# Gathering experts after four heads' choice instead of eight, with the weight remainders on VectorE

## What is computed

```
def peer_mixer(h, w_q, keys_1, keys_2, u_tab, v_tab):
    q = (hf @ w_q).reshape(t, PEER_HEADS, PEER_QUERY_DIM)
    s1 = jnp.einsum('thd,nd->thn', q[..., :half], keys_1)
    s2 = jnp.einsum('thd,nd->thn', q[..., half:], keys_2)
    v1, i1 = lax.top_k(s1, PEER_TOPK)
    v2, i2 = lax.top_k(s2, PEER_TOPK)
    cand = (v1[..., :, None] + v2[..., None, :]).reshape(t, PEER_HEADS, PEER_TOPK * PEER_TOPK)
    sc, ci = lax.top_k(cand, PEER_TOPK)
    ...
    experts = (e1 * PEER_N_KEYS + e2).reshape(t, PEER_HEADS * PEER_TOPK)
    gates = jax.nn.softmax(sc, axis=-1)
    def expert_block(args):
        a = jax.nn.gelu(jnp.einsum('td,ted->te', hb, u_tab[eb]), approximate=False)
        w = (gb * a)
        return jnp.einsum('te,ted->td', w, v_tab[eb])
```

## Time and profile before

| what | value |
|---|---|
| median of 3 runs | 2500.1 us (2497.99 to 2506.24) |
| the profiled execution | 2501.13 us, its span 2499.4 us |
| mean granted TensorE clock | 0.914 |
| busy, share of the span | PE 82%, DVE 63%, POOL 50%, ACT 40% |
| DMA | 726.60 MB, of which 540.59 MB by the indirect queue |

### The profile page before, as it was taken

How to read it: one execution, slowest core, us unless ns; L and a number is a source line. 1 busy time by engine, 2 the same in 40 slices (tenths; PEclk the granted TensorE clock), 3 DMA queues, 4 the chain that set the end, 5 groups by cost and what they waited for, 6 DMA issues and landing times. The chain is left out here.

```text
span 2499.4 us, 22306 instructions
## 1 busy us (share of the span) xinstructions
PE 2057.0 (82%) x7187; PEld 1278.5 (51%) x7187; DVE 1575.2 (63%) x2938; ACT 992.7 (40%) x2294; POOL 1251.8 (50%) x800
## 2 busy tenths in 40 slices
PE   5997867378999777777699888888999969687999
PEld 3785645244554232322356444445665647455787
DVE  4648546888886577765779875667887852452111
ACT  4215443133333222223453568445343334344443
POOL 3532000075765353444477444567898847004887
PEclk8986678689999899999899999899999989788999
DMA  7630035299999999999899999999999955003564
GB/s 263 232 121 1 1 133 152 93 419 406 420 420 405 421 421 421 422 421 421 350 358 377 409 404 344 377 378 380 419 418 407 418 208 155 26 1 93 171 191 153
DMA packets 128640, 726.60 MB, mean 291 GB/s; under 512 B 14471, under 2 KB 15498, under 8 KB 62986
## 3 DMA queue, kind: packets, MB, share of 16 engines
q0 software_dynamic: 74800, 540.59, 53.0%
q1 hardware_dynamic: 53088, 184.44, 21.2%
q10 hardware_dynamic: 634, 0.14, 0.0%
HBM read 716.45 MB, written 8.66 MB: 290 GB/s over the span
## 5 line engine op out<-in xcount | busy, mean ns | idle before, releaser
L1326 PE MATMUL ps<-uv_ring_a,expert_diag_a 128*128 128x512 f32 x1920 | 918.0, 624 | 232.9 <-ACT expert_diag_a L1308 214.6
L1107 POOL DMA_INDIRECT uv_ring_a<-in_peer_uv_dram,expert_idx x512 | 620.3, 1212 | 647.1 <-PE ps L1326 510.9
L1254 DVE CUSTOM_DVE_ANT_0 uv_ring_a<-uv_ring_a,x_rows 128x1024 f32<-128x1024 f32 x512 | 787.1, 1544 | 248.4 <-DMA uv_ring_a<-in_peer_uv_dram,expert_idx 246.8
L1326 PEld LDWEIGHTS ps<-uv_ring_a,expert_diag_a 128*128 128x128 f32 x1920 | 368.9, 198 | 699.9 <-issue 369.4
L1401 POOL TENSOR_TENSOR w_low_a<-w_raw_a,w_high_a 128x1024 fp32r<-128x1024 f32 x122 | 302.1, 2477 | 109.9 <-ACT w_high_a L1393 108.0
L1401 POOL TENSOR_TENSOR w_low_b<-w_raw_b,w_high_b 128x1024 fp32r<-128x1024 f32 x98 | 233.9, 2390 | 228.5 <-ACT w_high_b L1393 227.1
L1293 ACT ACTIVATE expert_gelu_a<-expert_dot_a 128x2 f32<-128x2 f32 x256 | 52.1, 204 | 691.0 <-DVE expert_dot_a L1254 690.7
L1393 ACT CAST w_high_a<-w_raw_a 128x1024 fp32r<-128x1024 f32 x146 | 152.0, 1042 | 192.5 <-PE ps L1414 172.5
L1308 ACT ACTIVATE expert_diag_a<-ident,expert_weight_a 128x128 f32<-128x128 f32 x480 | 168.5, 395 | 0.6 <-ACT expert_weight_a L1299 0.4
L1393 ACT CAST w_high_b<-w_raw_b 128x1024 fp32r<-128x1024 f32 x98 | 102.9, 1051 | 116.8 <-PE ps L1414 114.5
L1299 ACT ACTIVATE expert_weight_a<-expert_gelu_a,expert_gate 128x1 f32<-128x1 f32 x512 | 122.9, 286 | 8.6
(11 more groups left out here) (463 smaller groups left out, 3334.5 us busy)
## 6 DMA issues: line engine op xcount, KB each, us to landing
w_raw_a<-in_w_gu_dram SPq DMA_DIRECT2D x44, 512.0 KB, 7.8
w_raw_b<-in_w_gu_dram SPq DMA_DIRECT2D x44, 512.0 KB, 3.6
w_raw_a<-in_w_peer_q_dram SPq DMA_DIRECT2D x32, 512.0 KB, 7.1
w_raw_a<-in_w_out_dram SPq DMA_DIRECT2D x24, 512.0 KB, 7.7
w_raw_a<-in_w_in_dram SPq DMA_DIRECT2D x24, 512.0 KB, 6.2
w_raw_b<-in_w_in_dram SPq DMA_DIRECT2D x24, 512.0 KB, 3.8
w_raw_a<-in_w_down_dram SPq DMA_DIRECT2D x22, 512.0 KB, 7.8
w_raw_b<-in_w_down_dram SPq DMA_DIRECT2D x22, 512.0 KB, 3.6
```

Source lines behind the costliest of these rows:

```text
L1107: pool.indirect_dma_start(out=self.ring[:, n % self.RING, :], out_offset=None, in_=K.uv, in_offset=bass.IndirectOffsetOnAxis(ap=K.idx[self ...
L1254: dve.tensor_tensor_reduce(u, u, self.h[b][:, :], 1.0, 0.0, ALU.mult, ALU.add, self.a[:, s:s + 1]).then_inc(self.s_dot, 1)
L1326: ins = nc.tensor.matmul(self.bank(half), self.diag[q % self.DIAGS][:, :], self.ring[:, n % self.RING, D + 512 * half:D + 512 * half + 512 ...
```

## The change

It has five pieces.

- **Choice in groups of four.** `HG` goes from 2 to 4. Ahead of the first dot product only heads 0 to 3 of block 0 are chosen, and their gates made. Heads 4 to 7 are chosen during the first slots (204 steps of choice over 100 slots in block 0, for those heads and the next block), their gates at slot 42. The exponential and the gates are made in halves.
- **Scores loaded behind weight tiles.** For block 1 the first score load is placed after the first weight tile of `tail_b`, the second at the place of slot 36.
- **`tail_b` starts 3 slots later**, at `at(6)`.
- **All remainders of the first stage on DVE.** The 122 tiles of L1401 leave POOL's queue, which then holds indirect DMAs alone.
- **The front.** ACT writes `h_high` in one pass from the normalised row; DVE makes `h` itself (`tensor_scalar`, L513 of the changed kernel) and then the remainder; PE waits slice by slice for column tile 0.

```diff
@@ Columns.turned @@
+            if ready:
+                pe.wait_ge(ready, k + 1)
...
@@ stage_front: scalar, tensor, vector @@
-                act.activation(K.hT[:, k, :], K.hT[:, k, :], ACT.Identity, scale=K.g1[:, k:k + 1],
-                               bias=shift[k]).then_inc(s_h, 1)
-                act.wait_ge(s_h, k + 1)
-                act.copy(hi[:, k, :], K.hT[:, k, :]).then_inc(s_hh, 1)
+                act.activation(hi[:, k, :], K.hT[:, k, :], ACT.Identity, scale=K.g1[:, k:k + 1],
+                               bias=shift[k]).then_inc(s_hh, 1)
...
-                    w.turned(pe, n, K.ps[n % 2][:, :], x)
+                    w.turned(pe, n, K.ps[n % 2][:, :], x, ready=None if n else s_hl)
...
+                dve.tensor_scalar(K.hT[:, k, :], K.hT[:, k, :], K.g1[:, k:k + 1], shift[k], ALU.mult, ALU.add).then_inc(s_h, 1)
+                dve.wait_ge(s_h, k + 1)
                 dve.tensor_tensor(lo[:, k, :], K.hT[:, k, :], hi[:, k, :].bitcast(F32), ALU.subtract).then_inc(s_hl, 1)
@@ Gather @@
-    G, DIAGS, HG = 2, 4, 2
+    G, DIAGS, HG = 2, 4, 4
...
-                yield max(self.at((r - 2) * SLOTS + 44 * (hg + 1) + 4), tail.end + 4.0 + hg)
-                sp.wait_ge(self.s_swf, self.GROUPS * (r - 1) + 2 * hg + 2)
+                if r == 1:
+                    yield self.at(36) if hg else self.start - 1.0
+                else:
+                    yield max(self.at((r - 2) * SLOTS + 44 * (hg + 1) + 4), tail.end + 4.0 + hg)
+                sp.wait_ge(self.s_swf, self.GROUPS * (r - 1) + hg + 1)
...
-        for n in range(self.GROUPS * per + 1):
-            yield tail.scored[min(n // per, self.GROUPS - 1)] + 0.25 * (n % per)
-            next(first, None)
-        yield tail.end + 11.0
-        gates(0)
+        for n in range(per):
+            yield tail.scored[1] + 0.25 * n
+            next(first)
+        yield tail.scored[1] + 0.25 * per + 2.0
+        gates(0, 0)
...
+                if b == 0:
+                    ahead, steps, over = chain(first, ahead), steps + per, 100
...
-            while done * 88 < steps * (s + 1) and done <= steps:
+            while done * over < steps * (s + 1) and done <= steps:
                 next(ahead, None)
                 done += 1
+            if s == 42 and b == 0:
+                gates(0, 1)
...
-            if s == 0:
-                act.wait_ge(self.s_gate, b + 1)
+            if s % self.WIDE == 0:
+                act.wait_ge(self.s_gate, self.GROUPS * b + s // self.WIDE + 1)
...
+            if g == 19:
+                exps(0, 1)
@@ stage_first @@
-            plan.us = g.at(3)
+            plan.us = g.at(6)
...
-            weave(rows_in(pool), g.pool(pool), W.lows(pool, dense))
+            weave(rows_in(pool), g.pool(pool))
...
-            weave(g.dve(dve), W.lows(dve, 0, dense), bias.dve(dve), half.dve(dve, begin + 80.0), *(n.dve(dve, [(s_later, 16)]) for n in ahead),
+            weave(g.dve(dve), W.lows(dve), bias.dve(dve), half.dve(dve, begin + 80.0), *(n.dve(dve, [(s_later, 16)]) for n in ahead),
```

More of the change, by code:

```diff
@@ L9 @@
 from contextlib import ExitStack
+from itertools import chain
 F32 = mybir.dt.float32
@@ L203, in lows, with turned @@
                                self.hi[n % self.SPLIT][:, :].bitcast(F32), ALU.subtract).then_inc(self.s_lo, 1)
-    def turned(self, pe, n, bank, x, cols=P):
+    def turned(self, pe, n, bank, x, cols=P, ready=None):
         hi, lo = (t[n % self.SPLIT][:, :].rearrange("p (k c) -> p k c", k=KD) for t in (self.hi, self.lo))
@@ L442, in _ @@
             for n in range(VG):
-                if n == 0:
-                    pe.wait_ge(s_hl, KD)
-                else:
-                    if n >= 2:
-                        pe.wait_ge(*out(n - 2))
+                if n >= 2:
+                    pe.wait_ge(*out(n - 2))
                 if n == A:
@@ L1018 @@
 class Gather:
-    G, DIAGS, HG = 2, 4, 2
+    G, DIAGS, HG = 2, 4, 4
     GROUPS = PEER_H // HG
+    WIDE = HG * TOPK
     def __init__(self, K, ctx, blocks, rows, start, us, banks, ring, share=0, own=0):
@@ L1184, in route @@
             dve.wait_ge(self.s_idx, self.GROUPS * r + hg + 1)
+            den = self.den[:, HG * hg:HG * hg + HG]
+            ch.link(dve.tensor_copy(den, top[:, :, 0:1].rearrange("p a b -> p (a b)")))
+            dve.tensor_tensor(top, top, den.unsqueeze(2).to_broadcast([P, HG, TOPK]), ALU.subtract).then_inc(self.s_d, 1)
             yield
-        top = self.top[:, :, :]
-        ch.link(dve.tensor_copy(self.den[:, :], self.top[:, :, 0:1].rearrange("p a b -> p (a b)")))
-        dve.tensor_tensor(top, top, self.den[:, :].unsqueeze(2).to_broadcast([P, PEER_H, TOPK]),
-                          ALU.subtract).then_inc(self.s_d, 1)
-        yield
     def dve(self, dve):
@@ L1194, in dve, with gates @@
         ch = Chain(dve, self.s_dve)
-        def gates(r):
-            dve.wait_ge(self.s_e, r + 1)
-            g = K.gate[self.blocks[r] % 2][:, :].rearrange("p (h a) -> p h a", h=PEER_H)
-            ch.link(dve.tensor_reduce(self.den[:, :], g, AX_X, ALU.add))
-            ch.link(dve.reciprocal(self.den[:, :], self.den[:, :]))
-            dve.tensor_tensor(g, g, self.den[:, :].unsqueeze(2).to_broadcast([P, PEER_H, TOPK]),
-                              ALU.mult).then_inc(self.s_gate, 1)
+        def gates(r, hg):
+            dve.wait_ge(self.s_e, self.GROUPS * r + hg + 1)
+            g = K.gate[self.blocks[r] % 2][:, self.WIDE * hg:self.WIDE * (hg + 1)].rearrange("p (h a) -> p h a", h=self.HG)
+            den = self.den[:, self.HG * hg:self.HG * (hg + 1)]
+            ch.link(dve.tensor_reduce(den, g, AX_X, ALU.add))
+            ch.link(dve.reciprocal(den, den))
+            dve.tensor_tensor(g, g, den.unsqueeze(2).to_broadcast([P, self.HG, TOPK]), ALU.mult).then_inc(self.s_gate, 1)
         def add(n):
@@ L1247, in dve @@
             if s == 0:
-                ahead = self.route(dve, ch, r) if r < len(self.blocks) else iter(())
                 routing, done = r < len(self.blocks), 0
-                steps = self.GROUPS * per + 1
+                ahead = self.route(dve, ch, r) if routing else iter(())
+                steps, over = self.GROUPS * per, 88
+                if b == 0:
+                    ahead, steps, over = chain(first, ahead), steps + per, 100
                 dve.wait_ge(self.tails[b // 2].s_h, 4)
@@ L1255, in dve @@
                                      self.a[:, s:s + 1]).then_inc(self.s_dot, 1)
-            while done * 88 < steps * (s + 1) and done <= steps:
+            while done * over < steps * (s + 1) and done <= steps:
                 next(ahead, None)
                 done += 1
+            if s == 42 and b == 0:
+                gates(0, 1)
             if s == 110 and routing:
-                gates(r)
+                for hg in range(self.GROUPS):
+                    gates(r, hg)
                 r += 1
@@ L1279, in act, with exps @@
         per = SLOTS // G
-        def exps(r):
-            act.wait_ge(self.s_d, r + 1)
-            act.activation(K.gate[self.blocks[r] % 2][:, :], self.top[:, :, :].rearrange("p a b -> p (a b)"),
+        def exps(r, hg):
+            act.wait_ge(self.s_d, self.GROUPS * r + hg + 1)
+            act.activation(K.gate[self.blocks[r] % 2][:, self.WIDE * hg:self.WIDE * (hg + 1)],
+                           self.top[:, self.HG * hg:self.HG * (hg + 1), :].rearrange("p a b -> p (a b)"),
                            ACT.Exp).then_inc(self.s_e, 1)
-        yield self.tails[0].end + 10.0
-        exps(0)
+        yield self.tails[0].scored[1] + 0.25 * (15 * self.HG + 8) + 1.0
+        exps(0, 0)
         r = 1
@@ L1309, in act @@
                                scale=self.w[:, i:i + 1]).then_inc(self.s_diag, 1)
+            if g == 19:
+                exps(0, 1)
             if g % per == 52 and r < len(self.blocks):
-                exps(r)
+                for hg in range(self.GROUPS):
+                    exps(r, hg)
                 r += 1
```

9 lines of the change are left out of this document (4 added, 5 removed).

## The result

The changed kernel took 2476.7 us (2468.14 to 2478.64), the kernel before 2499.1 on the same chip: ratio 0.991 (0.9888 to 0.9933), some 22 us faster. Six more executions of it (the run `again`) gave 2471.6 and 0.9896 (0.9873 to 0.9918). The forecast was 2467, its range 2440 to 2489.

The account below looks back on a forecast made before the run. The gather's transfers, at a ceiling of 421 GB/s, were taken to bound the stage, so only an earlier start or fuller stretches help. -8 - 20 + 3 - 5 - 3 = -33 from the median 2500.1 gave 2467 us, range 2440 to 2489.

Parts of the forecast that it names:

- The front: Before the first stage: tile 0 and everything behind it come sooner, -8 us, bounds -5 and -9.
- The start: Start of the gather: transfers full at about 468 instead of 500, -20 us, bounds -13 and -26.
- The first block: Slots where DVE also chooses heads and makes remainders: local jams, +3 us, bounds 0 and +20.
- The later remainders: Dense stretches from 1200 to 1725, remainders on DVE: -5 us, at best 43 us of PE's gaps go.
- The end: Last products of the stage, no longer slowed beside a remainder on POOL: -3 us, bounds 0 and -5.
- the dense stretches were POOL's doing: Rival, losses after 1200: some 25 us come back instead of 5; 2447, range 2435 to 2455, chance 0.17.
- DVE is not relieved: Slower rival, whole stage: dot products keep 1.5 us and remainders come on top; 2530, chance 0.06.
- The rival of a first block bound by DVE: First block, DVE busy 284 of 295 us: +20 instead of +3; 2484, range 2480 to 2492, chance 0.13.
- the no-change rival: Gather starts early, but first-block jams (+28) eat the start and the front's 8 us go; 2495, chance 0.04.
- The signs: Across the trace: tile 0 copied out near 58, dot product 1.23 us, DVE busy about 245 of the first 295.
- the mark of 400: First block: the forecast is wrong if transfers there fall under 400 GB/s.
- One mark of being wrong: DVE's queue: the forecast is wrong if DVE waits for `w_high_a` by more than some 40 us in all.

Follow-up runs that it names:

- choice_alone: The changed kernel without its front's piece and with the 122 later remainders still on POOL; ratio 0.9922 to the kernel before.
- lows_later: The changed kernel with each remainder from tile 24 on placed 2 us later in DVE's order; 2470.8 us, ratio 0.9883.
- lows_alone: The kernel before with only the 122 later weight remainders moved from POOL to DVE; ratio 0.9941.
- tail_at_3: The changed kernel with tail_b's dense work back at the place of slot 3 instead of 6; 2456.1 us, ratio 0.9822.

## Why the prediction came out as it did

The sum was -33 against -22 and -29 measured in the two runs of the kernel. The direction, the early start and the front were right. Of the other terms the first block was mis-sized, and the later remainders came to their size by luck.

- **The front, -8.** Right. 6.6 us in the profiles, 10 (6 to 14) in time. The `tensor_scalar` took 0.54, not 0.42, and the pace was 1.18 us a slice instead of 1.1.
- **The start, -20.** Right: -19.9 and -21.6 at slot 16. The first index came at 454.5, 133.0 after `keys_raw`; the forecast was 458.8 with the stage 8 us earlier, 130.9. About 2.5 us of the 20 are bytes of `tail_b` that were only put off (26.2 MB moved by slot 16 against 27.2).
- **The first block, +3.** The term that failed: from slot 16 to 128 the changed kernel gives back 9.1 and 11.2 us, inside the bounds of 0 and +20. The choice beside the gather is not what was costed too low by itself. With `tail_b` at slot 3 the same choice and the same remainders cost 1.2 us. What failed is the sentence that "`tail_b` three slots later" costs nothing: its place is worth 12 us at slot 128 and 0.7 to 0.9% of the time. A row of the kernel before spoke of it, and I had not used it: DVE's eight subtractions of `tail_b` stood ahead of the first dot product, and the change puts them among the dot products.

```profile
501.24 4.79 DVE L2353 TENSOR_TENSOR tail_turned_low_a<-mixT,tail_turned_high_a 128x256 fp32r<-128x256 f32 x8 [4.66 <-ACT tail_turned_high_a L2338]
505.96 1.21 DVE L1254 CUSTOM_DVE_ANT_0 uv_ring_a<-uv_ring_a,x_rows 128x1024 f32<-128x1024 f32 x1
```

- **The later remainders, -5.** The size is right (57 us lost instead of 64; 6.6 and 3.8 us gained between slots 128 and 511), but by luck, for the cause is mostly another. The remainders alone gain 0.6 us there, the groups of four heads alone 4.6, whatever the remainders do. In the first block, though, they help: `choice_alone`, which leaves them on POOL, loses 17.2 us from slot 16 to 128, the changed kernel 12.4 and 13.9.
- **The end, -3.** Between the last dot product and the last part stand 1.6 to 1.7 us less in the kernels without remainders on POOL (but for `lows_later`), and no less in those with. That is the lower half of the bounds.
- **The rivals.** That the dense stretches were POOL's doing is refuted by `lows_alone`. That DVE is not relieved, too: 1544 to 1220 ns. The rival of a first block bound by DVE, with +20, was the nearest: half of it came, and by `tail_at_3` not for DVE's load alone. The 2495 of the no-change rival does not follow from its terms: +28 in place of +3 and the front's 8 give 2500.
- **The signs.** Tile 0 at 57.4, dot product at 1.22, DVE busy 234 of 295, no remainder on POOL, 404 GB/s just above the mark of 400; the two dense stretches lost 39 us, of the 46 before. One mark of being wrong came true: DVE's waits for `w_high_a` came to 146 us for these tiles, where I had called more than 40 a refutation. The time was in the range all the same, and with the waits cut to 54 us in `lows_later` the stage was no shorter. That they cost the gather nothing is not shown, as said there.

That VectorE and GpSimd held each other up was weighed with the Trainium skill ("SBUF — State Buffer", section "Who interferes with whom"): a lock on a shared port pair, held for a whole instruction. The trace after agrees: with no remainder beside them, 512 dot products take what the undisturbed ones took before, 1220 ns against 1224. The rule on starved descriptors, which would have spoken against the move, names two-port modes, which `tensor_tensor` has not by that section. Yet the remainder does hold POOL's indirect DMAs, as one with two SBUF inputs does by the section's other rule, if the indirect DMA counts as a GpSimd instruction that reads SBUF:

```profile
640.93 1.22 DVE L1411 TENSOR_TENSOR w_low_a<-w_raw_a,w_high_a 128x1024 fp32r<-128x1024 f32 x1
641.10 1.86 POOL L1111 DMA_INDIRECT uv_ring_a<-in_peer_uv_dram,expert_idx  x1 [1.29 <-PE ps L1336]
```

In the changed kernel an indirect DMA beside which DVE does nothing takes 0.93 to 0.96 us (79 of them). One that starts while DVE makes a remainder ends 0.8 us after the remainder does, here at 642.96 behind 642.15: of the 47 with at least 0.15 us of the remainder left, 46 end 0.79 to 0.83 us behind it. Behind a dot product it is the same for 110 of 114, and before the change for 199 of 202. Over all, the indirect DMAs take 1129 ns each after the change and 1212 before. So each of these waits is at most one instruction of DVE long, and as POOL waits 907 us for PE's additions, they set nothing here.

## What to carry to other kernels

When a start is moved ahead, look at what stood in the old pause: work that was free there has to be moved ahead as well, and a plan's start that is shifted by "only" three slots deserves an experiment of its own. Relief of a busy engine is worth what the bound resource gets of it: 57 us less on DVE and 332 less on POOL were worth 1 us behind slot 16 in the kernel before, and 3 to 5 in the first block of the changed one, where DVE had more to do. Judge a wait by what the gather gains when it is gone, not by its sum, and see that the edit which removes it adds none elsewhere.

## What was not expected of the hardware

The same 616 products of the mixers were granted 0.64 to 0.75 of TensorE's full clock from one execution to the next, and took 149 to 138 us, against 8 to 25 us by which whole executions of one kernel differ. What a step of 5 us does could be read only from marks inside the trace.

The other thing is that VectorE's instructions with two SBUF inputs hold back GpSimd's indirect DMAs for what is left of the instruction, as shown above: 0.94 us undisturbed, up to 2.0 behind one.
